# Attention scores left in PSUM, the gate projected first, a weight block moved ahead: a two-layer hybrid step on one core

## The chip, the cores and the metric

The kernel runs on one core of one Trainium2 chip. A core has a matrix engine (TensorE, PE in the rows), a vector engine (VectorE, DVE), a scalar engine with an activation unit (ScalarE, ACT), a general engine (GpSimd, POOL) and a queue that issues most transfers (SyncE, SP). All work side by side and meet at semaphores. The metric is the device time of one execution in microseconds, the median of several runs.

## What is computed

Two trunk layers work on 128 context tokens and 256 latent tokens of 1024 channels. Each layer modulates the normed input, projects it once, runs three token mixers of eight heads each (RWKV-7 in both directions, neighbourhood attention, retention in both directions), merges them by gates, and ends with a gated ConvFFN. What the change touches is this:

```
def ada_modulation(cvec, w, b):
    m = jax.nn.silu(cvec) @ w + b
    return m.reshape(m.shape[0], 6, D_MODEL)

# dense_attention, of context tokens: softmax(q k^T * scale) v
# neighbourhood_attention, of latent tokens: local keys with a bias, context keys without
        bias = rpb[:, dr[None, :, None], dc[:, None, :]].astype(F32)
        s_loc = jnp.einsum('bqhd,bjwhd->bhqjw', q_r, k_r).astype(F32) * scale + bias[None]
        s_loc = jnp.where(col_valid[:, None, :], s_loc, NEG_BIG).reshape(B, H, GRID_W, kh * GRID_W)
        s_ctx = jnp.einsum('bqhd,bhld->bhql', q_r, k_ctx).astype(F32) * scale
        p = jax.nn.softmax(jnp.concatenate([s_loc, s_ctx], axis=-1), axis=-1).astype(v.dtype)
        o = jnp.einsum('bhqn,bnhd->bqhd', p[..., :kh * GRID_W], v_r.reshape(B, kh * GRID_W, H, D))
        return o + jnp.einsum('bhql,bhld->bqhd', p[..., kh * GRID_W:], v_ctx)

# retention_branch, last step, g being the gate's projection
    o = (head_groupnorm(y, RET_GN_EPS) * lp['ret_gn'].astype(F32)).astype(z.dtype) * jax.nn.silu(g)
```

## The kernel before

**Data and weights.** The tokens lie transposed in the core's memory, as eight tiles of 128 channels by 386 columns (128 context, 2 of gap, 256 latent). All weights come as blocks of 128x1024 (512 KB) in one fixed order through a ring of five slots; SP issues block b once PE and ACT are done with block b-5 (L461). For the projections a block is used in three products at reduced precision: `split` on ACT copies it to `whi` (tile names in the rows: whi<-ring, 128x1024), `low` on POOL takes the rest in two subtractions of 128x512 (ringlo), and `three` on PE multiplies hi by hi, lo by hi and hi by lo. One `dense` is eight such triples, 24 matmuls of 386 columns.

**A layer.** It starts with the modulation rows: sixteen blocks `ADA0` to `ADA0 + 15` are multiplied by the conditioning of both streams (two columns, tile `small`), each block in four matmuls, in four column groups of the array, of 256 columns each; `sum_squares(0)` on PE adds up the squares for the norm. ACT copies the rows (`mod_rows`), PE transposes them (`mod_turned`), ACT modulates. Then come four pairs of heads. The late blocks of a pair (eight, the modulation for the layer's second half) are multiplied in small portions between other work: `ada_steps(n)` is 2n matmuls of 256 columns. `late_rows` on ACT copies their result.

**A pair** projects nq, nk, nv (attention), rq, rk, rv, rg (retention; rg is its gate, which ACT puts through Silu), and works through RWKV's inversion in levels lv = 1 to 5, in which PE alternates with masks and transposes on DVE. Attention and retention are laid between these levels by hand. The r, k and v of the next pair (here r', k', v') are projected ahead: `next_steps(n)` does n triples of them. Results of projections go to two banks of PSUM in turn (`z(zi)`); `opened` waits until the bank's last reader has freed it.

**Attention** handles six jobs a pair, (head, kind), kind 0 being context queries (128 keys) and kinds 1 and 2 latent ones (384 keys). For job j: `scores_mm(j)` on PE into bank w(4); ACT copies the context part to `scores`; DVE adds the bias while it moves the local part there, takes the maximum and its negative; ACT takes Exp and the sum (`powers`); DVE takes the reciprocal and scales the rows; `flip_mm(j)` on PE transposes them into w(5) (`tr`, L487); ACT copies them to `ptr`; `values_mm` multiplies by the values; ACT copies the output (`values`, tile `mix`). `attend(i)` issues flip_mm(i - 2) and scores_mm(i). PE, ACT, DVE and POOL each run their instructions in the order in which the program writes them, and that order is written by hand.

## Time and profile before

| | |
|---|---|
| median of 3 runs | 2035.76 us (2035.27 to 2041.24) |
| profiled execution | 2040.7 us |
| its span, first to last instruction | 2038.9 us |
| mean granted clock of PE | 0.965 |
| weight blocks issued | 400 of 512 KB |

The rows ahead of the prediction come from the profiled execution, whose own time is 4.9 us above the median of the runs; 1.8 us of it lie outside the span. Of an engine's row in a timeline the first number is the start from the beginning of the span, the second its duration, xN how many instructions it holds, and the bracket at its end how long the engine was idle before it and what ended that. A 32-bit matmul has two records in the profile.

### The profile page before, as it was taken

The numbers are of one execution on the slowest core, as the hardware profiler recorded it, in microseconds if no ns is written. First come the engines' busy times: TensorE is split into PE (matmuls) and PEld (weight loads), VectorE is DVE, ScalarE is ACT, GpSimd is POOL, SyncE is SP. The second block draws the span as 40 slices with busy tenths as digits, with TensorE's granted clock in tenths as the row PEclk, the third lists the DMA queues.
The fourth block names the chain that finished last, engine by engine and source line by source line (L and its number), as shares of the span: only waits on it lengthen the run. The fifth ranks groups of instructions, "written<-read, shape, count | busy, mean of one in ns | idle before, by whom it ended". The sixth has DMA issues, their size and how long they took to land.

```text
span 2038.9 us, 42069 instructions
## 1 busy us (share of the span) xinstructions
PE 1867.9 (92%) x18068; PEld 1681.3 (82%) x18068; DVE 1031.9 (51%) x1596; ACT 947.0 (46%) x1798; POOL 933.0 (46%) x767
## 2 busy tenths in 40 slices
PE   5889989898999989999978898989989998999997
PEld 2867878686999969999947687777869997899997
DVE  2574747566621255552056757484755133555502
ACT  3554545455433454444355555454554334544432
POOL 1433426161466536666516152442515664466663
PEclk8999999999999989999989999999999999999998
DMA  7314233232334314434353231423224342244342
GB/s 289 101 48 132 79 98 113 95 103 94 114 125 125 115 62 124 124 124 127 124 207 123 81 108 49 140 70 121 86 88 146 124 125 92 92 126 124 124 125 73
DMA packets 66568, 231.54 MB, mean 114 GB/s; under 512 B 7504, under 2 KB 13008, under 8 KB 65744
## 3 DMA queue, kind: packets, MB, share of 16 engines
q1 hardware_dynamic: 59040, 215.21, 32.8%
q10 hardware_dynamic: 7344, 13.66, 2.0%
q8 instruction: 143, 2.34, 0.5%
q14 instruction: 41, 0.34, 0.1%
HBM read 223.58 MB, written 5.26 MB: 112 GB/s over the span
## 4 chain that ended last, share of the span: by engine, by line
PE 79%; DVE 9%; ACT 4%; DMA 4%; POOL 2%; issue 1%; SPq 0%; ACTq 0%; DVEq 0%
PE psz L479 61%; PE psw L479 16%; DMA ring<-in_w 4%; DVE work L1441 2%; ACT work L997 2%; POOL ringlo L1846 2%; DVE work L1457 2%; DVE work L1453 1%; PE psz L487 1%; PE psw L487 1%; DVE work L1447 1%; ACT whi L997 1%; DVE work L1444 1%; DVE rstd L1450 1%; ACT L997 1%
## 5 line engine op out<-in xcount | busy, mean ns | idle before, releaser
L1846 POOL TENSOR_TENSOR ringlo<-ring,whi 128x512 fp32r<-128x512 f32 x608 | 806.4, 1349 | 747.8 <-ACT whi L997 747.8
L479 PE MATMUL psz<-hhi,whi 128*128 128x386 f32 x1696 | 592.8, 350 | 31.9 <-POOL ringlo L1846 23.3
L479 PE MATMUL psz<-hhi,ringlo 128*128 128x386 f32 x1696 | 577.7, 341 | 1.5 <-issue 1.5
L479 PE MATMUL psz<-hlo,whi 128*128 128x386 f32 x1696 | 578.3, 341 | 0.0
L997 ACT ACTIVATE whi<-ring 128x1024 fp32r<-128x1024 f32 x304 | 320.4, 1055 | 170.9 <-PE psz L479 124.5
L479 PEld LDWEIGHTS psz<-hhi,whi 128*128 128x128 f32 x1696 | 322.0, 190 | 52.6 <-issue 29.8
L479 PE MATMUL psz<-part,whi 128*128 128x386 f32 x1344 | 346.7, 339 | 3.1 <-DVE work L1441 1.7
L479 PE MATMUL psw<-work 64*64 64x64 f32 (+4 forms) x9024 | 303.8, 243 | 35.3 <-DVE work L1453 21.0
L479 PEld LDWEIGHTS psz<-hlo,whi 128*128 128x128 f32 x1696 | 323.5, 191 | 2.7
L479 PEld LDWEIGHTS psw<-work 64*64 64x64 f32 (+2 forms) x9024 | 248.1, 146 | 92.8 <-issue 48.4
L479 PEld LDWEIGHTS psz<-hhi,ringlo 128*128 128x128 f32 x1696 | 321.6, 190 | 0.0
L479 PEld LDWEIGHTS psz<-part,whi 128*128 128x128 f32 x1344 | 245.2, 189 | 4.3 <-issue 2.3
L479 PE MATMUL psz<-part,ringlo 128*128 128x386 f32 x672 | 227.5, 339 | 0.0
L997 ACT ACTIVATE work<-psw 128x128 f32<-128x128 f32 (+6 forms) x320 | 119.8, 415 | 185.1 <-PE psw L479 169.5
L1441 DVE TENSOR_TENSOR mix<-mix 128x386 f32<-128x386 f32 x68 | 86.9, 1277 | 193.8 <-ACT mix L997 192.4
L1846 POOL TENSOR_TENSOR work<-work 128x386 f32<-128x386 f32 (+1 forms) x48 | 45.8, 961 | 297.7 <-ACT work L997 296.0
L997 ACT ACTIVATE work<-psz 128x386 f32<-128x386 f32 (+4 forms) x224 | 95.8, 440 | 181.3 <-PE psz L479 171.3
L1447 DVE SCALAR_TENSOR_TENSOR mix<-psz,prm,mix 128x385 f32<-128x385 f32 x168 | 104.1, 619 | 133.7 <-ACT mix L997 130.5
L1441 DVE TENSOR_TENSOR work<-work 128x386 f32<-128x386 f32 (+2 forms) x184 | 155.8, 871 | 5.0
L997 ACT ACTIVATE mix<-psz,prm 128x386 f32<-128x386 f32 x84 | 49.1, 585 | 193.1 <-DVE mix L1441 100.1
L479 PEld LDWEIGHTS psz<-part,ringlo 128*128 128x128 f32 x672 | 126.3, 188 | 0.0
L1441 DVE TENSOR_TENSOR work<-psz,work 128x386 f32<-128x386 f32 x48 | 26.8, 558 | 187.7 <-PE psz L479 186.5
(107 smaller groups left out, 1725.8 us busy)
## 6 DMA issues: line engine op xcount, KB each, us to landing
ring<-in_w SPq DMA_DIRECT2D x400, 512.0 KB, 3.6
pk<-in_pk ACTq DMA_DIRECT2D x8, 640.0 KB, 4.0
const<-in_const SPq DMA_DIRECT2D x1, 1795.0 KB, 9.7
work<-in_x SPq DMA_DIRECT2D x1, 1544.0 KB, 6.7
work<-in_x ACTq DMA_DIRECT2D x1, 1544.0 KB, 7.9
out_x<-work ACTq DMA_DIRECT2D x1, 1544.0 KB, 7.5
work<-out_x ACTq DMA_DIRECT2D x1, 1544.0 KB, 7.2
out_x<-work SPq DMA_DIRECT2D x4, 386.0 KB, 2.4
```

Of the source, the lines that this page charges most:

```text
L479: ins = nc.tensor.matmul(out, a, b, start=start, stop=stop, skip_group_check=True)
L487: ins = nc.tensor.transpose(out, a, ident)
L997: L.do(nc.scalar.activation(out, src, f, **kw), S[sig] if sig else None, free)
L1441: L.do(V.tensor_tensor(out, a, b, op), *sig_of(sig, free))
L1444: L.do(V.tensor_scalar(out, a, s1, s2, op0, op1), *sig_of(sig, None))
L1447: L.do(V.scalar_tensor_tensor(out, a, s_, b, op0, op1), *sig_of(sig, free))
L1450: L.do(V.reciprocal(out, a), *sig_of(sig, None))
L1453: L.do(V.copy_predicated(out, mask, data), S[sig] if sig else None)
L1457: L.do(V.transpose(out.rearrange("p h x c -> p (h x c)"), a.rearrange("p h x c -> p (h x c)")), S[sig] if sig else None)
L1846: L.do(G.tensor_tensor(out, a, b, op), S[sig] if sig else None)
```

## The change

**Start.** A modulation block is multiplied by two matmuls of 512 columns in two column groups; each half of the array serves eight of the sixteen blocks, and `row_done` comes for the first two rows after eight blocks. The eight tiles of the squares are laid one behind each block from block 4 on (block 8 in layer 1).

**Attention.** The scores stay in PSUM. ACT's copy of the context part, DVE's addition of the bias, the separate negation and the scaling of the rows go. PE adds the bias by a matmul of the identity with the bias (128x256) into the bank; DVE takes the negated maximum from the bank; ACT's Exp reads the bank. DVE's reciprocal of the sum goes to ACT, which scales an identity by it (`rdiag`, one tile); the flip becomes a matmul with `rdiag`.

**Order.** rg is projected ahead of rk and rv, and ACT does its Silu ahead of the first Exp. In the weight stream the next pair's r block stands ahead of the last two late blocks; the ada_steps and next_steps between the stages are dealt out anew. On ACT `values(1)` goes ahead of `powers(3)`, and `late_rows` moves from behind the copies of u to behind `next_tap(0)`.

```diff
-    SPLIT += range(PAIR0 + PAIR_BLOCKS * _p, PAIR0 + PAIR_BLOCKS * _p + 10)
+    SPLIT += [PAIR0 + PAIR_BLOCKS * _p - 2 * (_p > 0), *range(PAIR0 + PAIR_BLOCKS * _p + 1, PAIR0 + PAIR_BLOCKS * _p + 10)]
...
-                    for b in range(2 * KT):
-                        if b == (10 if layer else 6):
-                            sum_squares(0)
-                        jp, k = divmod(b, KT)
-                        loaded(b)
-                        for j in range(4):
-                            mm(psw[32 * j:32 * j + 2, 1, 256 * jp:256 * jp + 256], cs[:, k, :],
-                               ring2[b % RING][:, j // 2, 256 * (j % 2):256 * (j % 2) + 256], k == 0, k == KT - 1,
-                               "row_done" if b == 2 * KT - 1 else None)
-                        used[0] += 1
+                    for jp in range(2):
+                        for k in range(KT):
+                            b = ADA0 + KT * jp + k
+                            loaded(b)
+                            for i in range(2):
+                                j = 2 * jp + i
+                                mm(psw[32 * j:32 * j + 2, 1, :], cs[:, k, :], ring2[b % RING][:, i, :], k == 0,
+                                   k == KT - 1, "row_done" if k == KT - 1 else None)
+                            used[0] += 1
+                            i = b - ADA0 - (KT if layer else KT // 2)
+                            if 0 <= i < KT:
+                                sum_squares(0, (i,))
...
-                                pe.wait_ge(*at_of("s_ready", p, j - 1))
+                                pe.wait_ge(*at_of("p_ready", p, j - 1))
...
-                                mm(w(4, P, 256), q, nk[rows(hb), LAT:TP], sig="sc_done")
+                                mm(w(4, P, 256), q, nk[rows(hb), LAT:TP], True, False)
+                                if j == 1:
+                                    pe.wait_ge(*at_of("bias_ready", p, 0))
+                                a = PK["bias"] + 384 * hb + (P if kind == 1 else 0)
+                                mm(w(4, P, 256), ident, pk[:, a:a + 256], False, True, "sc_done")
...
-                            pe.wait_ge(*at_of("pn_ready", p, j))
+                            pe.wait_ge(*at_of("ridiag_ready", p, j))
...
-                                tr(w(5, i * P, P), scores[j % 2][:, i * P:(i + 1) * P], "pt_done" if i == n - 1 else None)
+                                mm(w(5, i * P, P), scores[j % 2][:, i * P:(i + 1) * P], rdiag,
+                                   sig="pt_done" if i == n - 1 else None)
...
-                        dense(zb + ZI["rk"], bb + 7)
+                        dense(zb + ZI["rg"], bb + 7)
                         attend(0)
-                        dense(zb + ZI["rv"], bb + 8)
-                        dense(zb + ZI["rg"], bb + 9, between=lambda: attend(1))
+                        dense(zb + ZI["rk"], bb + 8)
+                        dense(zb + ZI["rv"], bb + 9, between=lambda: attend(1))
...
                             elif lv == LEVELS - 1:
-                                ada_steps(4)
+                                ada_steps(2)
...
                         retain(2)
-                        ada_steps(2)
+                        if p + 1 == PAIRS:
+                            ada_steps(4)
                         next_steps(2)
...
-                            if n < 2:
+                            if n == 0:
                                 next_steps(3)
+                            if n == 1 and p + 1 < PAIRS:
+                                ada_steps(4)
                             if n == 1:
                                 retain(3)
-                        next_steps(2)
...
                         retain(5)
-                        next_steps(3)
+                        next_steps(6)
                         pe.wait_ge(*at_of("ysq_ready", p, 0))
                         mm(w(3), blk, ysq, sig="gn_done")
-                        next_steps(4)
+                        next_steps(6)
...
-                            if i < 6:
-                                act.wait_ge(*at_of("sc_done", p, i))
-                                run(scores[i % 2][:, 0:P], w(4, 0, P), sig="sctx_ready")
+                            if 1 <= i <= 6:
+                                j = i - 1
+                                act.wait_ge(*at_of("ri_ready", p, j))
+                                run(rdiag, ident, ACT.Copy, "ridiag_ready", scale=ri[:, j % 2:j % 2 + 1])
...
-                                s_ = scores[i % 2][:, 0:384 if JOBS[i][1] else P]
-                                run(s_, s_, ACT.Exp, "p_ready", bias=mx[:, i % 2:i % 2 + 1], accum_out=rs[:, i % 2:i % 2 + 1])
+                                n = 384 if JOBS[i][1] else P
+                                run(scores[i % 2][:, 0:n], w(4, 0, n), ACT.Exp, "p_ready", bias=mx[:, i % 2:i % 2 + 1], accum_out=rs[:, i % 2:i % 2 + 1])
...
+                        values(1)
                         powers(3)
-                        values(1)
...
-                        late_rows(p, zb + ZI["ada"])
                         split(sb_ + 11)
...
                         next_tap(0)
+                        late_rows(p, zb + ZI["ada"])
                         retain(4)
...
-                                recip(ri[:, j % 2:j % 2 + 1], rs[:, j % 2:j % 2 + 1])
-                                L.settle()
-                                ts(s_[:, 0:n], s_[:, 0:n], ri[:, j % 2:j % 2 + 1], sig="pn_ready")
+                                recip(ri[:, j % 2:j % 2 + 1], rs[:, j % 2:j % 2 + 1], "ri_ready")
...
-                                    tt(s_[:, P:384], w(4, P, 256), pk[:, a:a + 256], ALU.add)
-                                    L.settle()
-                                n = 384 if kind else P
-                                L.do(V.tensor_reduce(mt[:, 0:1], s_[:, 0:n], AX.X, ALU.max), S["s_ready"])
-                                L.settle()
-                                ts(mx[:, i % 2:i % 2 + 1], mt[:, 0:1], -1.0, sig="mx_ready")
+                                dve.wait_ge(*at_of("sc_done", p, i))
+                                L.do(V.tensor_reduce(mx[:, i % 2:i % 2 + 1], w(4, 0, 384 if JOBS[i][1] else P), AX.X, ALU.max,
+                                                     negate=True), S["mx_ready"])
...
-            seq.append(wi[[p, 4 + p, 8 + p, 14 + p, 18 + p, 22 + p, 26 + p, 30 + p, 34 + p, 38 + p]])
-            seq.append(late[8 * p:8 * p + 8])
+            n = 0 if p == 0 else 1
+            seq.append(wi[[p, 4 + p, 8 + p, 14 + p, 18 + p, 22 + p, 26 + p, 38 + p, 30 + p, 34 + p][n:]])
+            if p + 1 < PAIRS:
+                seq += [late[8 * p:8 * p + 6], wi[[p + 1]], late[8 * p + 6:8 * p + 8]]
```

The diff leaves out `values(0)`, the copies and waits that follow the new order of rg, rk and rv on ACT, the lists of names, and the layout of the modulation weights, which now holds whole rows of 512 columns.

On PE at the start of a layer, `ring,small` are the modulation blocks and `mix,const` the squares:

```order
-L479 MATMUL psw<-ring,small 2x256 x24
-L479 MATMUL psw<-mix,const 128x386 x8
-L479 MATMUL psw<-ring,small 2x256 x40
+L479 MATMUL psw<-ring,small 2x512 x10
+L479 MATMUL psw<-mix,const 128x386
+L479 MATMUL psw<-ring,small 2x512 x2
+L479 MATMUL psw<-mix,const 128x386
+L479 MATMUL psw<-ring,small 2x512 x2
```

Before, twenty-four matmuls, the squares and forty matmuls; now the squares stand one by one between pairs of wide ones.

On PE in levels 3 and 4 of the inversion, `const,work` at L487 are transposes, flips into `psw`; `pk,const` is the bias:

```order
 L479 MATMUL psw<-work 64x128 x2
 L479 MATMUL psw<-work 64x64 x24
-L487 MATMUL psw<-const,work 128x128
+L479 MATMUL psw<-work 128x128
 L479 MATMUL psw<-pk,work 128x128
 L479 MATMUL psw<-work 128x256
+L479 MATMUL psw<-pk,const 128x256
 L487 MATMUL psz<-const,work 128x128 x6
 L479 MATMUL psw<-work 64x64 x24
```

A flip of either kind becomes a plain matmul, and the bias comes behind the scores.

On PE in the late stage of a pair, `hhi,whi`, `hlo,whi` and `hhi,ringlo` are one triple of the next pair's projections, `ring,small` the late modulation:

```order
 L479 MATMUL psz<-hhi,ringlo 128x386
 L479 MATMUL psw<-work 64x64 x8
-L479 MATMUL psz<-hhi,whi 128x386
-L479 MATMUL psz<-hlo,whi 128x386
-L479 MATMUL psz<-hhi,ringlo 128x386
-L479 MATMUL psz<-hhi,whi 128x386
-L479 MATMUL psz<-hlo,whi 128x386
-L479 MATMUL psz<-hhi,ringlo 128x386
-L479 MATMUL psz<-hhi,whi 128x386
-L479 MATMUL psz<-hlo,whi 128x386
-L479 MATMUL psz<-hhi,ringlo 128x386
+L479 MATMUL psz<-ring,small 2x256 x8
 L479 MATMUL psw<-work 64x128
```

Three triples give their place to eight modulation matmuls, which is `ada_steps(4)`.

On ACT in level 3, before, from the copy of output 3 on:

```order
L997 ACTIVATE mix<-psw 64x128 [waits no_done]
L997 ACTIVATE work<-psw 128x768 [waits gl_done]
L997 ACTIVATE work<-psw 128x384 [waits pt_done]
L997 ACTIVATE work<-psz 128x384 [waits z_done] x2
L997 ACTIVATE work<-work 128x384 [waits dt_ready] x2
L997 ACTIVATE small<-const,small 128x1 x4
L997 ACTIVATE mix<-psw 64x128 [waits no_done]
L997 ACTIVATE work<-psw 128x768 [waits gl_done]
```

And now:

```order
L1006 ACTIVATE mix<-psw 64x128 [waits no_done]
L1006 ACTIVATE work<-psw 128x768 [waits gl_done]
L1006 ACTIVATE work<-psw 128x384 [waits pt_done]
L1006 ACTIVATE work<-const,small 128x128 [waits ri_ready]
L1006 ACTIVATE work<-psz 128x384 [waits z_done] x2
L1006 ACTIVATE work<-work 128x384 [waits dt_ready] x2
L1006 ACTIVATE small<-const,small 128x1 x4
L1006 ACTIVATE mix<-psw 64x128 [waits no_done]
L1006 ACTIVATE work<-psw 128x768 [waits gl_done]
```

A copy of the identity that waits for DVE's reciprocal stands ahead of the bank copies, the two Exps on the decay tables and the copy of output 4.

## Rows read from the trace of the kernel before

**Rows 1.** The page: busy time, share of the span and instructions by engine.

```profile
PE 1867.9 (92%) x18068; PEld 1681.3 (82%) x18068; DVE 1031.9 (51%) x1596; ACT 947.0 (46%) x1798; POOL 933.0 (46%) x767
```

**Rows 2.** Waits of PE: line, what it waited for, total us, times, longest.

```profile
PE psw L479 <- DMA ring<-in_w: 25.3, 19, 10.1
PE psz L479 <- POOL ringlo L1846: 23.3, 14, 2.3
...
PE psw L487 <- ACT mix L997: 16.7, 8, 2.1
```

**Rows 3.** Windows of pair 1, then of pair 2, from flip(2) on.

```profile
core 0: us, PE busy (x) PEld busy (x) DVE busy (x) ACT busy (x) POOL busy (x), PEclk, DMA share, GB/s
...
246.20:257.80 11.60, 10.88 (x176) 8.31 (x176) 6.88 (x16) 7.40 (x20) 0.00 (x0) 0.71 0.01 4
...
360.80:370.90 10.10, 9.29 (x177) 7.10 (x177) 6.95 (x17) 7.41 (x20) 0.00 (x0) 0.83 0.01 3
```

**Rows 4.** Windows after pair 0's wait for Silu and after pair 1's for r'.

```profile
122.30:130.30 8.00, 7.97 (x122) 6.07 (x124) 4.84 (x9) 5.13 (x14) 0.00 (x0) 0.79 0.24 83
281.90:288.90 7.00, 7.00 (x155) 6.49 (x156) 1.02 (x2) 2.11 (x6) 2.51 (x2) 0.59 0.26 80
```

**Rows 5.** Timeline of PE at the start: start us, us, instructions, idle before.

```profile
10.10 1.03 PE L479 MATMUL psw<-ring,small 128*2 128x256 f32 x8 [10.10 <-DMA ring<-in_w]
...
16.37 1.03 PE L479 MATMUL psw<-ring,small 128*2 128x256 f32 x8 [0.23 <-DMA ring<-in_w]
17.34 7.94 PE L479 MATMUL psw<-mix,const 128*128 128x386 f32 x16
25.20 1.91 PE L479 MATMUL psw<-ring,small 128*2 128x256 f32 x32
...
37.94 1.03 PE L479 MATMUL psw<-ring,small 128*2 128x256 f32 x8 [0.45 <-DMA ring<-in_w]
...
51.71 0.45 PE L479 MATMUL psw<-hhi,whi 128*128 128x386 f32 x1 [2.88 <-DVE hlo L1441]
```

**Rows 6.** Window of layer 1's start, columns as in rows 3.

```profile
1021.10:1047.20 26.10, 17.85 (x145) 5.29 (x144) 13.16 (x19) 8.40 (x16) 0.00 (x0) 0.84 0.76 268
```

**Rows 7.** Timeline of PE in pair 1 of layer 0.

```profile
233.85 0.92 PE L479 MATMUL psz<-work,pk 128*128 128x386 f32 x2 [1.51 <-ACT work L997]
...
246.22 0.52 PE L487 MATMUL psw<-const,work 128*128 128x128 f32 x3 [2.09 <-ACT mix L997]
...
258.74 0.55 PE L487 MATMUL psw<-const,work 128*128 128x128 f32 x3
259.13 0.82 PE L487 MATMUL psz<-const,work 128*128 128x128 f32 x6
...
264.53 1.03 PE L479 MATMUL psw<-work,const 128*128 128x256 f32 x4
...
279.68 0.61 PE L479 MATMUL psz<-ring,small 128*2 128x256 f32 x8
281.87 0.66 PE L479 MATMUL psz<-hhi,whi 128*128 128x386 f32 x1 [1.57 <-POOL ringlo L1846]
```

**Rows 8.** Timeline of DVE in the same stretch.

```profile
234.98 0.42 DVE L1444 TENSOR_SCALAR work<-work,small 128x384 f32<-128x384 f32 x1
236.07 0.43 DVE L1441 TENSOR_TENSOR work<-psw,pk 128x256 f32<-128x256 f32 x1 [0.67 <-ACT work L997]
...
244.39 0.16 DVE L1450 RECIPROCAL small<-small 128x1 f32<-128x1 f32 x1
...
261.66 0.15 DVE L1450 RECIPROCAL small<-small 128x1 f32<-128x1 f32 x1
```

**Rows 9.** Timeline of ACT in the same stretch.

```profile
232.01 1.28 ACT L997 ACT_TABLE_LOAD   x1
...
259.98 0.88 ACT L997 ACTIVATE work<-psz 128x384 f32<-128x384 f32 x2
...
261.77 0.52 ACT L997 ACTIVATE work<-work 128x384 f32<-128x384 f32 x1 [0.46 <-DVE work L1447]
...
280.54 1.56 ACT L997 ACTIVATE work<-psz 2x256 f32<-2x256 f32 x4
...
300.44 1.05 ACT L997 ACTIVATE whi<-ring 128x1024 fp32r<-128x1024 f32 x1
```

More of the change, by code:

```diff
@@ L263, in trunk @@
         st = wk(3 * 256).rearrange("p (n s d v) -> p n s d v", n=3, s=2, d=2)
-        fin = wk(2 * 64).rearrange("p (d v) -> p d v", d=2)
+        rdiag = wk(P)
         lwal, lgl = wk(TP), wk(TP)
@@ L559, in keep_warm, with sum_squares @@
                             mm(w(3, 0, 256), ones, const[:, 0:256])
-                    def sum_squares(j):
-                        for k in range(KT):
+                    def sum_squares(j, tiles=range(KT)):
+                        for k in tiles:
                             pe.wait_ge(*after("sq_ready", KT * j + k + 1))
@@ L574, in ada_late @@
                         zb = ZP + 3 + ZPP * p
-                        b = PAIR0 + 3 + PAIR_BLOCKS * p + 7 + k
+                        b = PAIR0 + 3 + PAIR_BLOCKS * p + 7 + k + (k >= 6 and p + 1 < PAIRS)
                         if i == 0:
@@ L1226, in _ @@
                         run(vt, w(0, 0, 384).rearrange("p (t c) -> p t c", t=3), sig="vt_ready")
-                        seen(zb + ZI["rk"])
                         attend(0)
-                        powers(0)
+                        seen(zb + ZI["rg"])
                         if p:
                             act.wait_ge(*at_of("ro_ready", p - 1, 0))
+                        run(tg, z(zb + ZI["rg"]), ACT.Silu, free=zb + ZI["rg"])
+                        powers(0)
+                        seen(zb + ZI["rk"])
                         run(tk, z(zb + ZI["rk"]), free=zb + ZI["rk"], scale=0.125)
+                        attend(1)
+                        powers(1)
                         seen(zb + ZI["rv"])
                         run(mixed[2][p], z(zb + ZI["rv"]), free=zb + ZI["rv"])
-                        attend(1)
-                        powers(1)
-                        seen(zb + ZI["rg"])
-                        run(tg, z(zb + ZI["rg"]), ACT.Silu, free=zb + ZI["rg"])
                         seen(zb + ZI["rvt"])
```

27 lines of the change are left out of this document (10 added, 17 removed).

## The prediction

> **What bounds the kernel now.** The page's busy shares come first: PE is busy 92% of the span, DVE 51%, ACT and POOL 46% [rows 1]. So an instruction added on PE lengthens the run unless it lies ahead of a wait, and one removed from DVE or ACT gives time only where PE waits for it. The waits of PE say where: 25.3 us for weight blocks, 23.3 us for POOL's low parts, 16.7 us in eight waits of attention's flips for ACT's output copy [rows 2]. The change touches all three.
>
> My yardstick is head pair 1 of layer 0, read in stretches [rows 3]; six of eight pairs (0 to 2 of each layer) are built like it, and the last pair of a layer has no next pair to work ahead for. In 246.2 to 257.8 the granted clock averages 0.71, and the same stretch of pair 2 took 10.1 us at 0.83, not 11.6: a half-clock stretch of 3.4 us more costs about 1.5 us. Four of the eight pairs are like the one here, four like the other. The clock falls in two more places: after the wait for r' and, in pair 0 of each layer, after the wait for Silu [rows 4].
>
> **Start.** A block's four matmuls took 1.03 us at half clock, and six of them came in 7.24 us, 1.2 to 1.3 apart, by DMA; at full clock four blocks took 1.91 us, 0.48 each [rows 5]. Now two matmuls of twice the columns run side by side instead of four: by those rows at most twice as long, 0.95 at full and 1.8 at half clock (a little under twice 1.03, as part of it is fixed). At half clock that is more than the DMA's pace, so PE should be busy without a break from 10.10. Before, the clock rose only within the squares from 17.34: sixteen records took 7.94, where the start's half clock would have made it 10.2 and the full one 5.2. Four blocks at half clock (7.2), then twelve blocks (11.4) and eight squares at full clock (5.2) end at 33.9; before, the last block ended at 38.97 [rows 5]. That is -5; the sixteenth block frees its slot as much earlier, and the wait of 2.88 behind it, for the third dense block [rows 5], shrinks, so I take -7 (ends: -3.5, and -8). Layer 1 ran its blocks and squares in 26.1 us, 18 of them busy [rows 6]; 16 x 0.95 + 5.2 + some 2.5 of waits is 23: -3 (-2.5 to -3.7). Sum -10.
>
> **Attention, PE.** Four bias matmuls of 128x256: two such take 1.03 in the rope, with the way to their ends [rows 7], so some 0.45 each. Fourteen flips become matmuls: three transposes are 0.55 by themselves and 0.39 to the next start [rows 7], 0.13 each, and a 128x128 matmul by half the rope's is 0.24; +0.11 each. Together 3.3 us a pair. What lies ahead of a wait that ends elsewhere is hidden.
> - Up to flip(2): the wait of 1.51 for Silu goes (ACT loads a table, 1.28, first [rows 7, 9]); in its place PE waits for ACT's copy of rv, 0.5 and the way there, 0.65: -0.85. Bias and flip(0) add 0.55. DVE loses a scaling (0.42) and a bias (0.43) [rows 8], so that the masks start some 0.5 sooner: -0.4. Net **-0.7**. The wait of 2.09 at flip(2) [rows 7] I keep: ACT's output copy came behind the Exp that waited for DVE; now it comes behind the scaled identity, whose reciprocal DVE does only after its transposes, at 244.39 [rows 8], and in ACT's order two g copies and the output copy stand behind it. One wait takes the other's place.
> - From flip(2) to the next flip: PE busy 10.88 of 11.60, so all lies on the path: bias and three flips, +0.75; half of it at half clock, **+1.25**. The next level: bias and one flip, **+0.55**.
> - Level 3: DVE's scaling (0.42) goes, but the reciprocal of job 5 stands behind the decay tables and comes at 261.66 [rows 8], and on ACT the scaled identity stands ahead of two bank copies, two Exps on the tables, four small ones and output copy(4) (0.88, two of 0.52 and 1.1 for the rest [rows 9]). ACT did the bank copies at 259.98, before it had to wait; now they begin at 262.1, and copy(4) comes at about 265, where flip(5) starts 0.4 ahead of the rope's 264.53 [rows 7]. A new wait of 1.3 less what DVE gives back: **+0.5** (-0.35 to +1.5).
>
> **r' and late modulation.** PE waited 1.57 here for r''s low part (DMA issued behind the last late blocks, split 1.06, low parts 2.5 [rows 7, 9]); other pairs' 1.18 to 1.70. With the block two places ahead it lands before PE comes: -1.5. Two of its modulation steps (0.61 [rows 7]) also go from there: **-2.1**. After this wait PE ran at half clock for most of 7 us once (clock 0.59 [rows 4]) and for 3.4 us in three more of the six; half of such a stretch is lost, on average **-1.3**. The four steps come back later as **+0.95**.
>
> **Late stage.** k' opens its bank only when ACT's rows of late modulation have left it. They took 1.56 at 280.54, with much time; now they follow the tap and the split that end at 301.5 [rows 9], so at 303.05, and PE is there at 302.2 by its order (it has two fewer triples, 0.53 each, and 0.95 of steps ahead): +1.0 (0 to 1.0). The square for the group norm stands behind tap(1) and a split, 0.58 + 1.05 [rows 9] + 0.53 after k' is ready; PE has two triples, 1.06, as cover, and had seven: +1.0 (0 to 1.0). With the steps' 0.95: **+2.95** (0.95 to 2.95).
>
> **Sum.** A middle pair: -0.7 + 1.25 + 0.55 + 0.5 - 2.1 - 1.3 + 2.95 = +1.15, six +6.9. A last pair: -0.7 + 1.25 + 0.55 + 0.5 and 0.35 of steps that lose their cover: +1.95, two +3.9. Start -10. In each layer's pair 0 the half-clock stretch after the wait for Silu (0.79 over 8 us [rows 4], 1 lost beside what lies ahead of waits) goes: -2. New half-clock stretches after level 3's wait, in four of ten cases, 1.2 each: +3.8. Flips that now work as matmuls end a low clock sooner: -2. Sum +0.6 on the profiled 2040.7 (span 2038.9, 1.8 outside), which stands 4.9 over the median of the runs, 2035.76; on the median **2036.4**.
>
> **The rule on transposes.** 246.7 to 250.1 is full of work and still stayed at half clock in four of eight pairs (one of either kind in [rows 3]); four tenths of its time were transposes. The Trainium skill, "TensorE: Matmul & The Clock Gate", Part 4, says of transpose mode that it "doesn't count as PE-busy the same way"; the trace agrees. By that rule the change would bring more than its PE work suggests, which is rival 1.
>
> **Rivals.**
> 1. The flips as matmuls count: the second half-clock stretch after flip(2) goes where it stood (four pairs x 1.5) and level 3's never comes (3.8, less my 2): -8, 2028. For it: pair 2's 10.1 against 11.6. Against: six transposes in that stretch stay as they are. Chance 0.20.
> 2. The late waits are hidden (ACT or DVE run ahead of their place now): -2.0 x 6, 2024. For it: the late rows take 1.56 of ACT's time, and the queue ahead of them may be done sooner. Against: they stand behind the split. 0.15.
> 3. Slower: ACT's order decides. Copy(4) waits behind the reciprocal and level 3 takes its +1.5, and the clock falls after it in most pairs and again at k': 8 x 1.0 + 6 x 0.8 = +13, 2049. It decides from a wait of over 1 us at flip(5). 0.15.
> 4. Slower: at the start the clock stays low. Then a block with its square takes 1.8 + 1.3 = 3.1 us, the start ends at 42 to 48, +9 instead of -7, and +6 instead of -3 in layer 1: 2061. For it: the low blocks at 81% busy left it low. 0.07.
> 5. The change does not remove flip(2)'s wait, r''s wait merely moves to q' (its DMA now needs r' done), +0.7 x 8, 2042. 0.05.
>
> **How the numbers follow.** My forecast has 0.38, with its own range 2029 to 2044. A measurement tells some 0.3% (6.1 us) from no change: below 2029.7 is faster, over 2041.9 slower. Rival 1 gives 0.12 faster and 0.08 same; rival 2 0.14 and 0.01 same; rival 3 0.14 slower and 0.01 same; rivals 4 and 5 0.10 slower and 0.02 same; the forecast 0.06 faster, 0.26 same, 0.06 slower: 0.32, 0.38, 0.30. The range leaves out rival 4 and the far parts of 1, 2 and 3: 2021 to 2049.
>
> **What would show it.** Right: PE's start ends near 34 with the clock up by 20; no wait at r'; a wait of about 1.9 still at flip(2) and a new one of 1 to 1.5 at flip(5), for ACT; two waits of 1 us, for ACT, at k' and at the group norm's second sum; the stretch from flip(2) 1.2 longer. Wrong: PE at half clock past 25 us; no wait at flip(5) or at k', and pairs at 108 us or less; or new low-clock stretches from 281 on.

## The result: 1.15% slower, outside the range

Timed beside the kernel before on one chip, the changed kernel took 2058.72 us (2056.47 to 2068.39, four executions) against 2036.24 us: a ratio of 1.0115 with a 95% interval of 1.0078 to 1.0151. The forecast was 2036.4 with a range to 2049; the direction slower had 0.30. Timed again in another session (run after_again, six executions) it gave 1.0115, 1.0095 to 1.0135. A time in us is a median, a ratio compares mean times, so a ratio is not exactly the quotient of two medians.

The page of the changed kernel, busy times and the chain that ended last, with its granted clock:

```profile
PE 1893.7 (92%) x18116; PEld 1694.8 (82%) x18116; DVE 996.4 (48%) x1468; ACT 946.3 (46%) x1798; POOL 939.4 (46%) x767
...
PE 81%; DVE 8%; ACT 6%; issue 2%; DMA 2%; POOL 1%; ACTq 0%; SPq 0%; DVEq 0%
```
```profile
core 0: 2054.6 us, clock 0.976
```

PE is busy 25.8 us more than in [rows 1], although it ran at half clock less: a mean clock of 0.965 over 2038.9 us is 143 us at half clock, 0.976 over 2054.6 is 99. In these two executions the change so ended some 44 us of half clock, or 22 us of work. Over all timed executions it is less: the mean is 134 us at half clock for the kernel before (80 executions) and 110 for the changed one (10), so 24 us, or 12 us of work. It was slower all the same.

The waits of PE (what it waited for: total us, times, longest) name the new one. Of [rows 2], the wait of L487 for ACT's mix is now that of L479, since flips are plain matmuls, and it has eighteen occurrences where there were eight and two:

```profile
PE psw L479 <- ACT mix L1006: 38.2, 18, 6.4
PE psw L479 <- DVE work L1463: 19.4, 30, 0.8
PE psz L479 <- POOL ringlo L1842: 15.2, 8, 2.3
PE psw L479 <- DMA ring<-in_w: 14.0, 7, 10.2
PE psw L479 <- DVE hlo L1451: 13.0, 6, 4.1
PE psw L479 <- ACT work L1006: 12.9, 20, 1.2
```

Pair 1 of layer 0 in the timeline of PE, the stretch of [rows 7]:

```profile
233.10 0.55 PE L487 MATMUL psz<-const,mix 128*128 128x128 f32 x3 [0.58 <-ACT mix L1006]
...
245.95 0.91 PE L479 MATMUL psw<-work 128*128 128x128 f32 x6 [1.91 <-ACT mix L1006]
...
254.68 0.70 PE L479 MATMUL psw<-pk,const 128*128 128x256 f32 x2
255.22 0.82 PE L487 MATMUL psz<-const,work 128*128 128x128 f32 x6
...
262.96 0.93 PE L479 MATMUL psw<-work 64*64 64x64 f32 x48 [0.82 <-DVE work L1463]
265.15 0.91 PE L479 MATMUL psw<-work 128*128 128x128 f32 x6 [1.26 <-ACT mix L1006]
265.89 1.03 PE L479 MATMUL psw<-work,const 128*128 128x256 f32 x4
...
279.70 0.45 PE L479 MATMUL psz<-hhi,whi 128*128 128x386 f32 x1
...
298.87 0.44 PE L479 MATMUL psz<-hhi,whi 128*128 128x386 f32 x1 [0.99 <-ACT work L1006]
...
306.71 0.92 PE L479 MATMUL psw<-work,const 128*128 128x386 f32 x2 [0.96 <-ACT work L1006]
```

One reads here, from top to bottom: the wait for Silu has become one of 0.58 for the copy of rv; flip(2) waits 1.91 (2.09 before); a bias takes 0.54 from its start to the next; flip(5) waits 1.26 for ACT's output copy 4; the wait at r' is gone; k' waits 0.99 for the late rows and the second group norm sum 0.96 for the square. Every wait of the forecast is there, within 0.1 us of its size. What failed is the size of the work and of the overlaps around them.

ACT in the same pair, around flip(2) and around flip(5), and DVE's two reciprocals:

```profile
244.49 0.40 ACT L1006 ACTIVATE work<-const,small 128x128 f32<-128x128 f32 x1 [3.57 <-DVE small L1460]
244.80 0.85 ACT L1006 ACTIVATE work<-psw 128x384 f32<-128x384 f32 x2
245.54 0.26 ACT L1006 ACTIVATE mix<-psw 64x128 f32<-64x128 f32 x1
...
262.00 0.40 ACT L1006 ACTIVATE work<-const,small 128x128 f32<-128x128 f32 x1 [1.64 <-DVE small L1460]
262.31 0.85 ACT L1006 ACTIVATE work<-psz 128x384 f32<-128x384 f32 x2
...
264.74 0.27 ACT L1006 ACTIVATE mix<-psw 64x128 f32<-64x128 f32 x1
```
```profile
244.29 0.16 DVE L1460 RECIPROCAL small<-small 128x1 f32<-128x1 f32 x1
...
261.80 0.16 DVE L1460 RECIPROCAL small<-small 128x1 f32<-128x1 f32 x1
```

ACT stands idle for 3.57 us and for 1.64 us with the scaled identity at the head of its queue, until DVE has come through its transposes or its decay tables to a reciprocal of 0.16 us. Behind that head stand g copies and an output copy whose inputs had long been there.

### The profile page after: what moved, and what is told of

The parts are those of the page before. It is cut to its first block, busy times and chain, and to the rows that moved or that the text cites. A ratio compares the mean times of both kernels' runs of the same rounds, so it can differ in the third digit from the quotient of the medians.

```text
span 2054.6 us, 42029 instructions
## 1 busy us (share of the span) xinstructions
PE 1893.7 (92%) x18116; PEld 1694.8 (82%) x18116; DVE 996.4 (48%) x1468; ACT 946.3 (46%) x1798; POOL 939.4 (46%) x767
## 4 chain that ended last, share of the span: by engine, by line
PE 81%; DVE 8%; ACT 6%; issue 2%; DMA 2%; POOL 1%; ACTq 0%; SPq 0%; DVEq 0%
PE psz L479 61%; PE psw L479 18%; ACT work L1006 3%; DVE work L1451 2%; DMA ring<-in_w 2%; DVE work L1463 2%; DVE work L1467 2%; PE psz L487 1%; ACT whi L1006 1%; POOL ringlo L1842 1%; DVE work L1457 1%; DVE rstd L1460 1%; ACT mix L1006 0%; DVE small L1457 0%; DVE work L1454 0%
## 5 line engine op out<-in xcount | busy, mean ns | idle before, releaser
L479 PE MATMUL psz<-hhi,whi 128*128 128x386 f32 x1696 | 591.6, 349 | 28.8 <-POOL ringlo L1842 15.2
L479 PE MATMUL psz<-hlo,whi 128*128 128x386 f32 x1696 | 577.1, 340 | 0.0
L479 PE MATMUL psz<-hhi,ringlo 128*128 128x386 f32 x1696 | 575.7, 339 | 0.0
L479 PE MATMUL psw<-work 64*64 64x64 f32 (+5 forms) x9248 | 327.8, 237 | 53.2 <-ACT mix L1006 25.4
L479 PEld LDWEIGHTS psw<-work 64*64 64x64 f32 (+3 forms) x9248 | 266.4, 140 | 115.8 <-issue 78.2
L479 PEld LDWEIGHTS psz<-hhi,whi 128*128 128x128 f32 x1696 | 321.0, 189 | 43.9 <-issue 16.4
L479 PE MATMUL psz<-part,whi 128*128 128x386 f32 x1344 | 346.7, 339 | 2.9 <-DVE work L1451 1.5
L479 PEld LDWEIGHTS psz<-hlo,whi 128*128 128x128 f32 x1696 | 322.9, 190 | 2.9
L479 PEld LDWEIGHTS psz<-hhi,ringlo 128*128 128x128 f32 x1696 | 320.7, 189 | 0.0
L479 PEld LDWEIGHTS psz<-part,whi 128*128 128x128 f32 x1344 | 245.2, 189 | 4.1 <-issue 2.1
L479 PE MATMUL psz<-part,ringlo 128*128 128x386 f32 x672 | 227.5, 339 | 0.0
L1006 ACT ACTIVATE work<-psw 128x384 f32<-128x384 f32 (+8 forms) x272 | 108.1, 440 | 126.9 <-PE psw L479 122.0
L1451 DVE TENSOR_TENSOR work<-work 128x386 f32<-128x386 f32 (+2 forms) x184 | 151.0, 845 | 5.0
L479 PEld LDWEIGHTS psz<-part,ringlo 128*128 128x128 f32 x672 | 126.3, 188 | 0.0
```

What stands on the lines that cost most here:

```text
L479: ins = nc.tensor.matmul(out, a, b, start=start, stop=stop, skip_group_check=True)
L1006: L.do(nc.scalar.activation(out, src, f, **kw), S[sig] if sig else None, free)
L1451: L.do(V.tensor_tensor(out, a, b, op), *sig_of(sig, free))
```

## The experiments

Every ratio below is to the kernel before in the same session on the same chip; "us" is the median. The four parts are disjoint sets of the diff's hunks and together give the changed kernel.

**The parts one by one.** only_A holds the hunks on attention (PSUM scores, bias and flips by matmul, `values(1)` ahead of `powers(3)`), only_R those on the stream, the steps and `late_rows`, only_G the order rg, rk, rv on PE and ACT and in the stream, only_S the start:

```diff
--- only_A, one of its hunks
-                                tr(w(5, i * P, P), scores[j % 2][:, i * P:(i + 1) * P], "pt_done" if i == n - 1 else None)
+                                mm(w(5, i * P, P), scores[j % 2][:, i * P:(i + 1) * P], rdiag,
+                                   sig="pt_done" if i == n - 1 else None)
--- only_R, one of its hunks
-            seq.append(late[8 * p:8 * p + 8])
+                seq += [late[8 * p:8 * p + 6], wi[[p + 1]], late[8 * p + 6:8 * p + 8]]
--- only_G, one of its hunks
-                        dense(zb + ZI["rk"], bb + 7)
+                        dense(zb + ZI["rg"], bb + 7)
--- only_S, one of its hunks
-                        if b == (10 if layer else 6):
-                            sum_squares(0)
+                            i = b - ADA0 - (KT if layer else KT // 2)
+                            if 0 <= i < KT:
+                                sum_squares(0, (i,))
```

> The kernel before with the attention part alone (scores in PSUM, bias by matmul, flips by matmul with the scaled identity, output copy 1 ahead of Exp 3 on ACT). Theory 1 (this part is the loss): in the trace of the changed kernel a pair spends 0.54 more on each of four biases and 0.13 more on each of fourteen flips, 2.0 us of it in the open from flip(2) to level 3, and waits 1.26 at flip(5) with 0.84 won back at the level 4 mask; that is +2.5 to +3.5 a pair, so +20 to +28 us in all, and a wait of 1.2 to 1.3 for ACT's output copy at flip(5) in all eight pairs. Rival (the loss is in the late stage and the start, attention pays for itself by fewer half-clock stretches): between -5 and +8 us.

> The kernel before with the stream and late stage alone (r' ahead of the last two late blocks, modulation and projection steps dealt out anew, late rows behind next_tap(0)). Theory 1: the wait at r' (1.2 to 1.7) and the half-clock stretches behind it go, two waits of 1.0 for ACT come at k' and at the second group norm sum; full-clock terms +1.5 a pair, clock -1.4 a pair: -4 to +4 us. Rival (the late stage is the loss): +10 us or more.

> The kernel before with the gate projected first and nothing else. Theory 1: the wait of 1.51 for Silu becomes one of 0.6 for ACT's copy of rv, so -0.9 a pair, and pair 0's half-clock stretch may go: -6 to -10 us. Rival (the Silu and its two table loads ahead of the first Exp push later work back): no change or slower.

> The kernel before with the start of a layer alone (512-column modulation matmuls, squares one behind each block). Theory 1: in the trace of the changed kernel layer 0's start is 3 to 5 us shorter, of which 2 remain behind the wait for the third dense block; layer 1's is no shorter, since the squares end only behind the blocks and the norm's root waits for them: -3 to +1 us. Rival, my prediction: -10 us.

| run | us | ratio, 95% interval |
|---|---|---|
| only_A | 2062.93 | 1.0135 (1.0107 to 1.0163) |
| only_R | 2030.22 | 0.9976 (0.9956 to 0.9996) |
| only_G | 2026.06 | 0.9956 (0.9941 to 0.9972) |
| only_S | 2031.89 | 0.9986 (0.9973 to 0.9999) |

The attention part is the whole loss, 27.5 us; its rival, that it pays for itself, falls. The late stage gains 5 us net of its two new waits, 1 more than its expectation allowed; the gate gains 9, as expected, and the start 3 and not 10. In only_A's list of waits the place is the same as in the whole, to the tenth:

```profile
PE psw L479 <- ACT mix L1002: 38.2, 18, 6.4
```

**Everything but attention.** no_A is the changed kernel with the hunks of only_A taken back.

```diff
--- after
+++ no_A
-                                mm(w(5, i * P, P), scores[j % 2][:, i * P:(i + 1) * P], rdiag,
-                                   sig="pt_done" if i == n - 1 else None)
+                                tr(w(5, i * P, P), scores[j % 2][:, i * P:(i + 1) * P], "pt_done" if i == n - 1 else None)
...
```

> The changed kernel with the attention part undone: start, gate first and late stage stay. Theory 1 (the parts add up, attention is the whole loss): 0.9976 x 0.9956 x 0.9986 = 0.992, so about 2019 us against 2035 of before; the wait of 2.1 at flip(2) is there in all pairs, none at flip(5). Rival (the parts get in each other's way, since 1.0115 of the whole is 1.0007 more than the product of the four): 2028 us or more.

2021.89 us, 0.9942 (0.9922 to 0.9961). Without attention the change makes the kernel faster, 1.7 points under the whole. Its time lies between theory 1 and its rival: the product of the three parts alone is 0.9918, just outside the interval of no_A, but that product has an uncertainty of 0.003 of its own, so this run does not show whether the three add up. For all four parts it is clear: their product is 1.0052 (the expectation above put it too near the whole), and the whole is 1.0115, 0.6 points or some 13 us more.

**Do parts get in each other's way?** A_and_R has those two parts alone.

```diff
--- only_A
+++ A_and_R
-            seq.append(late[8 * p:8 * p + 8])
+                seq += [late[8 * p:8 * p + 6], wi[[p + 1]], late[8 * p + 6:8 * p + 8]]
...
```

> The changed kernel as it is, timed again with more executions. If the parts add up (1.0135 x 0.9942 for attention and all the rest), 1.0076, 2050 us; if they get in each other's way, 1.0115 again, 2058 us.

> Attention part and late stage together, without the gate first and the start. If parts add up 1.0135 x 0.9976 = 1.011, 2057 us; if it is these two that get in each other's way (the late waits of 1.0 only come open behind the slower attention), 2064 us or more.

after_again gave 2062.80 us, 1.0115; A_and_R 2061.22 us, 1.0118 (1.0096 to 1.0140); the product of its parts, 1.0111, lies within that. So attention and the late stage add up, and what is lost lies with the gate and the start: 0.9942 by their product alone, nothing on top of the other two. No run has attention with the gate alone or with the start alone, so how the loss is shared is read from traces only. For the gate the trace tells why. It and the attention part shorten one and the same wait of PE, that of 1.51 for Silu. In only_A it is already down to 0.71, because ACT has no context scores to copy ahead of it; in only_G and in the whole it is 0.58, at the copy of rv. Timeline of PE in only_A, only_G and ACT's table load ahead of Silu in only_A:

```profile
239.03 0.92 PE L479 MATMUL psz<-work,pk 128*128 128x386 f32 x2 [0.71 <-ACT work L1002]
```
```profile
230.41 0.55 PE L487 MATMUL psz<-const,mix 128*128 128x128 f32 x3 [0.58 <-ACT mix L997]
```
```profile
237.19 1.28 ACT L1002 ACT_TABLE_LOAD   x1
```

From the last group norm sum to the matmul of g a middle pair takes 36.26 us before, 35.40 in only_G, 35.90 in only_A and 35.84 in the whole (half-clock time counted half).

**Transposes again.** after_tr keeps scores in PSUM and the bias matmuls, and flips by transpose with rows scaled on DVE.

```diff
--- after
+++ after_tr
-                                mm(w(5, i * P, P), scores[j % 2][:, i * P:(i + 1) * P], rdiag,
-                                   sig="pt_done" if i == n - 1 else None)
+                                tr(w(5, i * P, P), scores[j % 2][:, i * P:(i + 1) * P], "pt_done" if i == n - 1 else None)
...
-                                act.wait_ge(*at_of("ri_ready", p, j))
-                                run(rdiag, ident, ACT.Copy, "ridiag_ready", scale=ri[:, j % 2:j % 2 + 1])
...
+                                ts(s_[:, 0:n], s_[:, 0:n], ri[:, j % 2:j % 2 + 1], sig="pn_ready")
```

> The changed kernel with scores in PSUM and bias on TensorE, but flips as transposes again: DVE scales the rows after its reciprocal, ACT makes no scaled identity. Theory 1: flips give back 0.13 each, fourteen a pair, and ACT's output copy 4 no longer stands behind the reciprocal of job 5, so the wait of 1.26 at flip(5) goes: -2 to -2.5 a pair, 2039 to 2043 us. Rival (the bias matmuls, 0.54 each, are most of the loss and the flips nearly free): 2050 us or more.

2020.08 us, 0.9927 (0.9903 to 0.9952): 38 us (1.88 points) less than the changed kernel, where 18 were expected. The flip with a scaled identity is more than the whole loss. Two things are in it, the matmul and the wait, and the next run parts them.

**A matmul with a plain identity.** after_mmid is after_tr with `mm(..., ident)` in place of `tr`.

```diff
--- after_tr
+++ after_mmid
-                                tr(w(5, i * P, P), scores[j % 2][:, i * P:(i + 1) * P], "pt_done" if i == n - 1 else None)
+                                mm(w(5, i * P, P), scores[j % 2][:, i * P:(i + 1) * P], ident,
+                                   sig="pt_done" if i == n - 1 else None)
```

> Scores in PSUM, bias by matmul, rows scaled on DVE, and the flips as matmuls against the plain identity: against the same with transposes (2020 us) it differs by the matmul alone. Theory 1 (TensorE's work is the small part, the wait for ACT's scaled identity the large one): +0.13 x 14 a pair and what lies ahead of waits taken off, +8 to +14 us, 2028 to 2034. Rival (matmuls for flips cost the whole 38 us): 2050 or more. Rule on transposes (a matmul counts for the clock, a transpose not): less half-clock time than the 73.9 us there, and less than +8 us.

2026.83 us, 0.9956 (0.9940 to 0.9972): +6.7 us, a little under theory 1. So the matmul costs 7 of the 38 us, and 31 come with the exchange of DVE's scaling for ACT's scaled identity. For the rule on transposes: in the profiled executions the mean clock was 0.984 over 2026.3 us against 0.982 over 2019.6, 65 us against 73 at half clock, as the rule would have it. But over all executions the mean is 65 us here (7 executions) and 67 us in after_tr (6). A gain for the clock from flips as matmuls is not shown, and it is less than their own cost.

**The scaled identity's place.** after_r2 and after_r5 change nothing but where DVE does one reciprocal each; after_r2_r5 both.

```diff
--- after
+++ after_r2, after_r5, after_r2_r5
+                            if q == 1:
+                                scaled(2)            # after_r2: behind four of the six mask products
...
                             if lv == 2:
+                                scaled(5)            # after_r5: ahead of the decay tables
                                 for hb in range(2):
```

> The changed kernel with DVE's reciprocal 2 in the middle of its six mask multiplications and nothing else. Theory 1: the scaled identity 2 no longer holds back the g copies and output copy 1 on ACT, the wait of 1.91 at flip(2) goes in eight pairs and with it the half-clock stretches behind it: -15 to -25 us, 2034 to 2044. Rival (DVE's transposes decide level 1 anyway): -5 us or less.

> The changed kernel with DVE's reciprocal 5 ahead of its four decay table operations and nothing else. Theory 1: ACT does its bank copies two microseconds sooner, output copy 4 is early, the wait of 1.26 at flip(5) goes and some of it comes back at the masks: -4 to -12 us, 2047 to 2055. Rival: output copy 4 waits for ACT's six Exps in any case, no change.

> The changed kernel with DVE's reciprocals 2 and 5 both early, the late stage as it is. Theory 1 (the scaled identity's place in ACT's order is the loss, and the two waits are apart from one another): against the changed kernel -28 from the one and -20 from the other measured alone, so -40 to -48: 2010 to 2018 us. Rival (both gave the same clock relief, which is had only once): 2025 us.

| run | us | ratio, 95% interval |
|---|---|---|
| after_r2 | 2030.49 | 0.9981 (0.9969 to 0.9994) |
| after_r5 | 2037.99 | 1.0017 (1.0005 to 1.0030) |
| after_r2_r5 | 2015.62 | 0.9889 (0.9869 to 0.9908) |

Both are better than theory 1 had it, by 3.5 and 9 us beyond its range, and together they take 2.3% off, the sum of 1.3 and 1.0, as expected. after_r2_r5 is also 0.4 points under after_tr, so the place of the scaled identity, more than its work, made the loss. In after_r2 ACT, DVE and PE's waits read:

```profile
236.40 0.40 ACT L1006 ACTIVATE work<-const,small 128x128 f32<-128x128 f32 x1
237.15 1.02 ACT L1006 ACTIVATE work<-psw 128x384 f32<-128x384 f32 x2 [0.35 <-PE psw L479]
238.47 0.27 ACT L1006 ACTIVATE mix<-psw 64x128 f32<-64x128 f32 x1 [0.30 <-PE psw L479]
```
```profile
234.93 0.15 DVE L1460 RECIPROCAL small<-small 128x1 f32<-128x1 f32 x1
```
```profile
PE psw L479 <- ACT mix L1006: 22.9, 10, 6.4
```

The reciprocal is at 234.93, ACT goes straight on, output copy 1 is at 238.47, and the eight waits of 1.91 are gone (38.2 less 15.3 is 22.9). In after_r5 the other eight go:

```profile
PE psw L479 <- ACT mix L1006: 28.1, 10, 6.4
```

Why more than expected: the waits themselves are 15.3 and 10.1 us. The profiled execution of after_r2_r5 was granted 0.984 over 2018.2 us, 65 us at half clock against 99 in the changed kernel; over all executions it is 62 (4 executions) against 110. That is 17 us of work in the two profiled ones and 24 on average, and 24 with the waits of 25.4 make somewhat more than the 43 to 46 us measured. What went are the half-clock stretches behind flip(2) and flip(5): in the middle pairs, from flip(2) on, there were 31 us at half clock in the profiled execution of the changed kernel and none in that of after_r2_r5.

**All orders mended.** after_early also moves the late rows on ACT behind `split(sb_ + 12)` and a wait for r', and the square ahead of `next_tap(1)`; no_A_early and after_tr_early do the same to no_A (with `values(1)` ahead of `powers(3)`) and to after_tr.

```diff
                         split(sb_ + 12)
+                        if p + 1 < PAIRS:
+                            seen(zb + ZI["r"])
+                        late_rows(p, zb + ZI["ada"])
...
                         next_tap(0)
-                        late_rows(p, zb + ZI["ada"])
...
-                        next_tap(1)
                         act.wait_ge(*at_of("yc_ready", p, 0))
                         run(ysq, yc, ACT.Square, "ysq_ready")
+                        next_tap(1)
```

> The whole changed kernel with four orders mended: DVE's reciprocal 2 in the middle of the masks, reciprocal 5 ahead of the decay tables, late rows on ACT behind split(12) and a wait for r', the square for the norm ahead of next_tap(1). Theory 1 (the four waits are order, not work): the waits of 1.91, 1.26, 0.99 and 0.96 go, part of them to DVE's masks: -34 us at most, 2025 to 2035 us. Rival (other chains stand right behind these waits): less than -10 us.

> The changed kernel without its attention part, with the same four orders mended (DVE's reciprocal and row scaling in place of the reciprocal alone) and output copy 1 ahead of Exp 3 on ACT. Theory 1: 2019 us less 2.0 in eight pairs and 1.9 in six: 1992 to 2002 us. Rival: the wait at flip(2) moves to the masks and transposes of DVE, 2010 us or more.

> Scores in PSUM, bias by matmul, flips as transposes with DVE's row scaling, and the four orders mended (reciprocals 2 and 5 with their scalings early, late rows behind split(12), the square ahead of next_tap(1)). Theory 1: against 2020 it loses the waits of 0.9 at flip(2) and of 0.99 and 0.96 in the late stage: -7 and -12, 1998 to 2004 us; the kernel without the attention part had 1992.6 with the same orders, so scores in PSUM with a bias by matmul would then cost 6 to 11 us by its four matmuls. Rival (they pay for themselves): 1992 us or less.

| run | us | ratio, 95% interval |
|---|---|---|
| after_early | 2007.27 | 0.9862 (0.9835 to 0.9889) |
| after_tr_early | 2005.63 | 0.9858 (0.9842 to 0.9875) |
| no_A_early | 1992.56 | 0.9797 (0.9770 to 0.9825) |

after_early is 51 us under the changed kernel, where 34 at most were expected: its expectation counts the four waits alone, and half-clock time fell too, from 110 us to 60 in the mean over all executions. The rival, other chains right behind these waits, falls. Most of it is the two reciprocals; the two late orders on top of after_r2_r5 bring 8 us in the medians, 0.3 points, which the intervals do not separate from nothing. after_tr_early missed its expectation by 2 us. It and after_early are alike (0.9858 and 0.9862): once the orders are mended, a scaled identity with matmuls costs no more than DVE's scaling with transposes, as far as these runs can tell. The fastest is no_A_early, 2.0% under the kernel before: the change without its attention part. after_tr_early is 13 us slower (0.6 points, with some 0.3 of uncertainty), and what it has more is scores in PSUM with a bias by matmul: 32 biases of 0.54 are 17 us of PE's work. And no_A_early is 29 us under no_A: more than half of the 51 us is there without the attention part, so it is not all a cost of that part.

## Why the prediction was wrong

Of the rivals the third came nearest: ACT's order decides, from a wait of over 1 us at flip(5); it was 1.26. I had given it 2049 us and 0.15. Of the others, rival 1 (flips as matmuls count for the clock) does not show: only_A has 137 us at half clock in the mean of its four executions, the kernel before in the same session 133, and behind flip(2) a stretch of 6.8 us still stands in three of eight pairs of the changed kernel and in four of after_again. So the rule on transposes, with which I had the trace agree, is not borne out by these runs: the half-clock stretches it was read from came back with the flips as matmuls. Rival 4, a clock that stays low at the start, and rival 5, a wait moved to q', did not come.

**Attention, flip(2) to the rope: mis-sized.** That attention loses was in the forecast: its own terms there, eight times 2.45 a pair, +3.8 and -2, make 21 us, and only_A measured 27.5. The forecast had +0.75, +0.55 and +0.5 a pair at full clock, 1.8. From scores(4) behind flip(2) to the rope a pair takes, with half-clock time counted half, 14.5 us before and 17.3 in the changed kernel, +2.7. PE's own work was larger than I worked out. In the groups by form (count | busy, mean ns):

```profile
L479 PE MATMUL psw<-work 128*128 128x128 f32 x256 | 42.2, 294 | 25.4 <-ACT mix L1006 25.4
...
L479 PE MATMUL psw<-pk,const 128*128 128x256 f32 x64 | 25.8, 490 | 0.0
...
L487 PE MATMUL psw<-const,work 128*128 128x128 f32 x56 | 9.9, 282 | 4.3 <-ACT work L1006 4.3
```

the 32 biases are busy for 25.8 us, each 0.54 from its start to the next one's instead of 0.45, and the flips add 0.13, not 0.11 (these 128x128 groups held 38.0 us before and 52.1 now, over 112 flips). The larger part is level 3 and 4, forecast "+0.5": the wait of 1.26 is what I had worked out, but three flips of 0.12 more stand behind it in the open, and DVE's masks gave back 0.5, not 0.8: at level 4 PE waits 0.82 for them in place of 1.68, but 0.36 of that difference is the longer flips of job 4 ahead of this wait; +1.2 in place of +0.5. In all 0.9 a pair, 7 us. The wait of 1.68 in the kernel before:

```profile
263.28 0.93 PE L479 MATMUL psw<-work 64*64 64x64 f32 x48 [1.68 <-DVE work L1453]
```

**"One wait takes the other's place": right, and worth nothing where it could be worth much.** The wait at flip(2) stayed at 1.91. It took another form: before it stood behind an Exp, now behind a reciprocal of 0.16 us that DVE does last. `values(1)` now stands ahead of `powers(3)`, which could have ended the wait: in after_tr, where the scaled identity is gone, 0.9 is left of it, for DVE's scaling. I kept the half-clock stretches too, and that made the item dear: after_r2 is worth 28 us. Since this wait was there before the change (2.09), it does not explain the loss against the kernel before; the new wait is that at flip(5), and after_r5, which ends it, is worth 21 us.

**Gate first: right alone, wrong in the sum.** I took -0.85 a pair for the shorter wait and, as a further term, what attention takes from DVE. only_G gave -9 us, as forecast, but attention alone shortens the same wait by 0.8. Up to flip(2) the forecast was -0.7; measured is +0.2 (-0.4 ahead of g, +0.6 from g to scores(4)), again 7 us in eight pairs. It is the error that a sum over parts makes when two of them shorten one wait.

**r' and the late stage: right.** The wait at r' went, the waits of 0.99 and 0.96 came, the half-clock stretches behind r' went. From the rope to the last group norm sum of a pair a middle pair takes 44.9 us in place of 44.0 (half-clock time counted half), +0.9 where the forecast had +0.85. Alone the part gained 5 us; rival 2, that the two waits are hidden, falls. What they were worth is not shown clear of noise (after_early against after_r2_r5).

**The start: mis-sized, 7 us.** Forecast -10, measured -3 alone. Layer 0, timeline of PE:

```profile
10.20 7.07 PE L479 MATMUL psw<-ring,small 128*2 128x512 f32 x20 [10.20 <-DMA ring<-in_w]
17.21 0.92 PE L479 MATMUL psw<-mix,const 128*128 128x386 f32 x2
...
33.01 1.03 PE L479 MATMUL psw<-ring,small 128*2 128x512 f32 x4 [0.24 <-DMA ring<-in_w]
34.65 1.03 PE L479 MATMUL psw<-ring,small 128*2 128x512 f32 x4 [0.61 <-DMA ring<-in_w]
...
48.34 0.69 PE L479 MATMUL psw<-hhi,whi 128*128 128x386 f32 x1 [4.10 <-DVE hlo L1451]
```

The clock rose sooner than forecast: five blocks are done at 17.2, where the forecast had four, and by their spacing (1.7 us a block at first, 0.95 later) it rose at about 15.5. But a square behind a block takes 0.84 from start to start and not 0.65 (the trace of before, in layer 1, has two of them from 1019.56 to the next start at 1021.15, 0.80 each, which I did not use), and two of the last blocks wait 0.24 and 0.61 for their DMA, so the blocks end at 35.7, not 33.9; the third dense block then waits 4.10 instead of 2.88, and the clock falls in that wait. Of 4.9 us ahead of it 3.4 are left, and 2.8 behind the two shared blocks. In layer 1 the squares come last, and the norm hangs on them: PE's last square, ACT's root behind it, and PE's first dense matmul:

```profile
1050.89 0.92 PE L479 MATMUL psw<-mix,const 128*128 128x386 f32 x2
...
1062.36 0.44 PE L479 MATMUL psw<-hhi,whi 128*128 128x386 f32 x1 [3.46 <-DVE hlo L1451]
```
```profile
1051.84 0.58 ACT L1006 ACTIVATE rstd<-psw,small 128x386 f32<-128x386 f32 x1 [3.02 <-PE psw L479]
```

Before, the root had come at 1040.6, 6.6 us before the last block's rows; now it follows them. I priced the matmuls and not what waits for the squares. In the kernel before, PE's squares at full clock and ACT's root and first copy of the rows read:

```profile
1019.56 1.66 PE L479 MATMUL psw<-mix,const 128*128 128x386 f32 x4
1021.15 1.91 PE L479 MATMUL psw<-ring,small 128*2 128x256 f32 x32
```
```profile
1040.61 0.58 ACT L997 ACTIVATE rstd<-psw,small 128x386 f32<-128x386 f32 x1 [1.01 <-PE psw L479]
1047.17 0.59 ACT L997 ACTIVATE work<-psw 2x512 f32<-2x512 f32 x1 [5.98 <-PE psw L479]
```

**The clock: better than forecast in the profiled executions, not on average.** In the pairs the terms on it summed to -4 us (six times -1.3, -2, +3.8, -2, and 0.5 of each of eight +1.25). In the two traces some 14 us of work came back there, and 8 more at and between the starts, so 10 us better than forecast. But the mean over all executions is 12 us of work in all (134 against 110 us at half clock) and not 22. So on average the clock did about what was forecast, and the extra 10 us are luck of the two executions that were profiled. The relief came mostly with the start and the late stage: the mean half-clock time is 113 us in only_S, 117 in only_R, 131 in only_G and 137 in only_A, against 133 before. The -2 for flips as matmuls is shown by no run.

**The sum.** Between the two profiled executions the changed kernel is 15.8 us slower, where the forecast had 0.6: attention's path 7, the gate's overlap 7, the start 7, less 10 from the clock, make 11, and 4 stay unassigned. The medians are 22.5 apart, since the profiled execution of before was 4.9 above its median and that of the changed kernel 2.3 below. On the medians the 10 from the clock fall away: 21 us of three mis-sized terms and the forecast's 0.6 stand against 22.5. The split is worked out from single executions; what the runs show is the size of the parts and of the two waits for the scaled identity.

## What to carry to other kernels

Before a small step moves from one in-order engine to another, look at what stands behind it there: two reciprocals of 0.16 us, late in DVE's queue, held ACT, and ACT held PE; issuing them where their input is ready gave 2.3%. Not quite half of that was the new wait; the rest stood in the kernel before behind an Exp, so look at the old waits too. Work out the parts of a change as one set of waits, not as a sum of savings: two parts that shorten the same wait gain once. And a wait can cost more than its length, here 43 us for waits of 25, since half-clock stretches followed them, so a wait that "stays" is worth removing.

## What was not expected of the hardware

The same program's executions spread by up to 16 us (the kernel before: 2026.6 to 2042.8 over all sessions). Half-clock time differs between two profiled executions of the changed kernel: clock 0.976 over 2054.6 us and 0.974 over 2061.3 us, 99 and 109 us at half clock. What varies in the traces is whether a stretch behind a wait stays away, or runs 3.4 or 6.8 us at half clock. A single profiled execution therefore tells waits to 0.1 us and a total only to some 10; for the clock, take the mean over all executions.
